# Earlier start of a triangular inverse's upper levels, other places for score products, and zero products inside its steps

## The chip, the cores and the metric

The kernel is one program on one core of a Trainium2 chip. It uses TensorE (PE: matrix products, results into the banks ps0 to ps7 of PSUM), VectorE (DVE), ScalarE (ACT), GpSimd (POOL), and SyncE (SP), which here only issues DMAs. The metric is the device time of one execution in microseconds, as the median of the runs. Lower is better.

## What is computed

Two transformer blocks over 256 tokens of width 1024. The change touches the mixer of the first block only, which has an RWKV-7 half and an attention half (NSA). Their outputs are put side by side and projected. All arithmetic is fp32; a projection is split in high and low parts (three products for one).

```python
def step(S, inp):                      # RWKV-7, one token, 8 heads of 64
    r_t, w_t, k_t, v_t, a_t, b_t = inp
    sa = jnp.einsum('bhvk,bhk->bhv', S, a_t)
    S = S * w_t[:, :, None, :] + sa[..., None] * b_t[:, :, None, :] + v_t[..., None] * k_t[:, :, None, :]
    return S, jnp.einsum('bhvk,bhk->bhv', S, r_t)
...
k_cmp = compress(kc, pe_k, ck1, ck2)   # gelu(blk @ w1) @ w2, 15 blocks
v_cmp = compress(vc, pe_v, cv1, cv2)
...
return gb[..., 0:1] * o_c + gb[..., 1:2] * o_s + gb[..., 2:3] * o_w
```

The scan over tokens is done in two chunks of 128 tokens. Within a chunk it needs, for each head, the inverse of a unit lower triangular matrix of 128 by 128 made of products of keys: 16 of them, called units of the inverse.

## The kernel before

**Front part.** `w_in` (L764) runs the items of the first projection in the order of `IN_ITEMS`: column blocks 0 to 21, then `gate`, then the two token products `tok 0` and `tok 1`. A column block waits for `lo_blk`, which VectorE gives with `lo_block` (L2034) after ScalarE's cast of the same block. Near the end VectorE also makes the keys `bT` and `kT_` (L2194 to L2197, semaphore `ab_ready`).

**Score products.** `rwkv_A_first` (L820) makes the strictly lower part of all 16 matrices into four banks, `rwkv_A(p)` (L833) the rest for the pair p of heads (p from 0 to 7). VectorE reads them through a mask: `A_first` (L2268), then `A_rest(lo, hi)` (L2283), one read for each of 16 matrices. A pair can only be made when an earlier pair's banks have been read (`A_read`). A table `A_PAIRS` tells behind which items pairs are made.

**The inverse.** SP moves the diagonal blocks of 16 by 16 through DRAM into a layout where VectorE inverts all of them at once (`small_inverse`, L2292), and back: one DMA out, then eight in (`blocks_back`). Levels 4, 5 and 6 then join blocks to 32, 64 and 128 rows. That is done in twelve steps (`STEPS`: three levels, four groups of four matrices). A step q is: P, eight small products into ps0 (`rwkv_P`, L853); a copy of P by ScalarE (`P_ev`); dM, small products into ps1 (`dM_ps`); an update of M by VectorE (`M_ready`) and, at level 4, transposes of M (`Mt_ready`). P of step q+1 is issued right behind dM of step q.

**The attention** is 34 units, software-pipelined in `nsa(i)`. TensorE's `nsa(i)` issues the scores of unit i, the value product of unit i-3 and the transpose of unit i-2; VectorE adds the bias and takes the maximum of unit i (L2358); ScalarE takes the exponential of unit i-1 and copies the transpose of unit i-2. Units 0 to 16 have 128 keys (short), 17 to 33 have 256 (long). Units 8 and 25 are the compressed branch, and behind units 7, 8, 16, 24 and so on VectorE makes a result (L2317).

**The compression.** `compress` (L1019) makes the hidden layer, `compress_T` turns it, ScalarE applies Gelu in `compress_act` (L1592), TensorE makes compressed keys and values in `compress_out` (L1049), ScalarE copies them, and VectorE's `compress` (L2396) spreads the values (`Vbd`, `cmp_ready`). The first transpose of the attention on TensorE waits for `cmp_ready`.

**The order in `rwkv`** (L872, L1518, L2201) is written out by hand for each engine. TensorE: pairs 4 and 5, `compress_T`, pair 6, `nsa(0)`, pair 7, `compress_out`, five zero products, `nsa(1)` to `nsa(3)` with four zero products behind each, and then P of step 0 and the steps. `stay_busy` issues the zero products: the operand is zero, and nobody reads the result. `NSA_STEPS` tells how many `nsa` calls a step holds.

## Time and profile before

| | us |
|---|---|
| median of 3 runs | 1398.94 (1398.36 to 1399.71) |
| the profiled execution | 1398.15 |
| its span in the profile | 1396.3 |
| TensorE busy | 1368.1 |
| VectorE busy | 943.5 |
| ScalarE busy | 689.1 |

The times in the rows count from the start of the span. Each engine carries out its instructions in order. The rows are from one execution, the profiled one. "x16" in a row of PE counts records, of which an fp32 product has two.

### The profile page before, as it was taken

Reading aid. Unit: us, or ns where it says so; the run is one execution under the profiler, and the core shown is the slowest. Engines: PE = TensorE matmul, PEld = TensorE weight load, DVE = VectorE, ACT = ScalarE, POOL = GpSimd, SP = SyncE. Lnnn points to the kernel's source line nnn. Section 1 sums busy time; section 2 is a strip of 40 time slices with the busy share of each in tenths; the row PEclk is TensorE's granted clock in tenths of the full one; section 3 lists DMA queues with packets and bytes.
Section 4 is the critical chain, followed back from the end, with each engine's and each line's share of the span. In section 5 each row is a group of like instructions: output and inputs, shape, how many; then the busy total and the mean of one; then the engine's idle time right before and its main releaser. Section 6 shows DMA issues by size and latency. Waiting matters only on the chain. (4 is left out here: it accounts for less than half of the span.)

```text
span 1396.3 us, 25767 instructions
## 1 busy us (share of the span) xinstructions
PE 1368.1 (98%) x10188; PEld 1261.5 (90%) x10188; DVE 943.5 (68%) x1539; ACT 689.1 (49%) x1107; POOL 82.3 (6%) x137
## 2 busy tenths in 40 slices
PE   8999999999999999999999999999999999999997
PEld 8897788999989999899989999999998988899997
DVE  4778567766668666577577666676665676676665
ACT  6764545433454443376654433444433756643442
POOL 1031010000020000000000000100000123000000
PEclk9999999999999999999999999999999999999999
DMA  9355015655536555433356555365555423465540
GB/s 360 137 170 189 2 34 224 226 180 192 205 106 227 219 181 185 177 116 129 119 210 228 195 180 188 133 232 203 193 180 181 151 92 137 181 226 182 197 162 31
DMA packets 33070, 239.48 MB, mean 172 GB/s; under 512 B 6864, under 2 KB 13280, under 8 KB 14304
## 3 DMA queue, kind: packets, MB, share of 16 engines
q1 hardware_dynamic: 30320, 234.84, 46.4%
q10 hardware_dynamic: 2672, 3.58, 0.8%
q8 instruction: 52, 0.85, 0.2%
q14 instruction: 26, 0.21, 0.0%
HBM read 236.15 MB, written 2.25 MB: 171 GB/s over the span
## 5 line engine op out<-in xcount | busy, mean ns | idle before, releaser
L500 PE MATMUL ps<-uT_h,w_gu 128*128 128x256 f32 x3520 | 600.2, 277 | 2.1 <-ACT uT_h L1335 2.0
L500 PEld LDWEIGHTS ps<-uT_h,w_gu 128*128 128x128 f32 x3520 | 532.7, 188 | 12.8 <-issue 4.7
L500 PE MATMUL ps<-uT_l,w_gu 128*128 128x256 f32 x1760 | 474.6, 277 | 0.0
L500 PEld LDWEIGHTS ps<-uT_l,w_gu 128*128 128x128 f32 x1760 | 325.3, 188 | 0.0
L500 PE MATMUL ps<-w_dn,h_r 128*128 128x512 f32 x1320 | 320.4, 392 | 0.3 <-DVE h_r L2089 0.3
L500 PEld LDWEIGHTS ps<-w_dn,h_r 128*128 128x128 f32 x1320 | 239.7, 188 | 46.7 <-issue 1.5
L1387 ACT CAST w_gu<-ring 128x2048 fp32r<-128x2048 f32 x110 | 209.9, 1908 | 139.5 <-PE ps L500 139.1
L2047 DVE TENSOR_TENSOR w_gu<-ring,w_gu 128x2048 fp32r<-128x2048 f32 x110 | 252.1, 2292 | 35.0 <-ACT w_gu L1387 35.0
L1400 ACT ACTIVATE wk<-wk 128x256 f32<-128x256 f32 x110 | 46.0, 418 | 265.6 <-DVE wk L2078 265.5
L2080 DVE TENSOR_TENSOR us<-ps,bc 128x256 f32<-128x256 f32 x110 | 46.5, 422 | 185.5 <-PE ps L500 185.5
L1393 ACT CAST w_dn<-ring 128x1024 fp32r<-128x1024 f32 x110 | 115.7, 1052 | 76.3 <-PE ps L500 75.7
L2053 DVE TENSOR_TENSOR w_dn<-ring,w_dn 128x1024 fp32r<-128x1024 f32 x110 | 134.1, 1219 | 5.1 <-ACT w_dn L1393 4.9
L500 PE MATMUL ps<-uT_h,ring_r 128*128 128x256 f32 x408 | 113.2, 279 | 0.0
L500 PEld LDWEIGHTS ps<-uT_h,ring_r 128*128 128x128 f32 x408 | 77.0, 189 | 0.6 <-issue 0.2
L500 PE MATMUL ps<-wk 32*32 32x32 f32 (+8 forms) x648 | 70.9, 273 | 2.3 <-DVE small L2358 1.0
L2078 DVE TENSOR_TENSOR wk<-ps,bc 128x256 f32<-128x256 f32 x110 | 46.7, 425 | 34.2 <-PE ps L500 20.9
L500 PE MATMUL ps<-ring_r,uT_h 128*128 128x512 f32 (+2 forms) x176 | 61.7, 351 | 0.0
L500 PEld LDWEIGHTS ps<-wk 128*128 128x128 f32 (+4 forms) x648 | 48.7, 160 | 9.2 <-issue 2.6
L2083 DVE TENSOR_TENSOR wk<-wk,us 128x256 f32<-128x256 f32 x110 | 46.8, 425 | 8.0 <-ACT wk L1400 4.8
L500 PE MATMUL ps<-uT_h,in_h 128*128 128x256 f32 x176 | 49.6, 284 | 1.8 <-DVE ring_r L2040 1.7
L2089 DVE TENSOR_TENSOR h_r<-wk,h_r 128x256 fp32r<-128x256 f32 x110 | 46.8, 426 | 3.8
L500 PE MATMUL ps<-uT_l,in_h 128*128 128x256 f32 x176 | 47.8, 278 | 0.0
(397 smaller groups left out, 1693.3 us busy)
## 6 DMA issues: line engine op xcount, KB each, us to landing
ring<-wstream SPq DMA_DIRECT2D x144, 1536.0 KB, 6.3
cst<-consts_in SPq DMA_DIRECT2D x1, 2185.0 KB, 13.7
wk<-t_row ACTq DMA_DIRECT2D x1, 2048.0 KB, 8.1
wk<-masks_in SPq DMA_DIRECT2D x1, 1216.0 KB, 24.0
x<-x_in SPq DMA_DIRECT2D x2, 512.0 KB, 4.7
ring<-wstream SPq DMA_DIRECT2D x1, 1024.0 KB, 8.8
inh<-gains ACTq DMA_DIRECT2D x2, 512.0 KB, 9.9
tri_blocks<-wk SPq DMA_DIRECT2D x3, 256.0 KB, 2.8
```

The costliest lines, as they stand in the source:

```text
L500: return pe.matmul(o, l, r, start=start, stop=stop, skip_group_check=True)
L1387: act.copy(w_gu[:, c % 2, 0, :], slot(i)[:, 0:2 * D]).then_inc(s["hi_a"], 1)
L1393: act.copy(w_dn[:, c % 2, 0, :], slot(i)[:, 2 * D:3 * D]).then_inc(s["hi_b"], 1)
L1400: act.activation(sg[:, c % 2, :], sg[:, c % 2, :], ACT.Silu).then_inc(s["silu_ready"], 1)
L2047: v.tensor_tensor(w_gu[:, c % 2, 1, :], slot(i)[:, 0:2 * D], w_gu[:, c % 2, 0, :].bitcast(F32), ALU.subtract).then_inc(s["lo_a"], 1)
L2053: v.tensor_tensor(w_dn[:, c % 2, 1, :], slot(i)[:, 2 * D:3 * D], w_dn[:, c % 2, 0, :].bitcast(F32), ALU.subtract).then_inc(s["lo_b"], 1)
L2078: v.tensor_tensor(h, ps[4 + c % 2][:, 0:T], bc[:], ALU.mult).then_inc(s["gs_ready"], 1)
L2080: v.tensor_tensor(us[:], ps[6 + c % 2][:, 0:T], bc[:], ALU.mult).then_inc(s["us_ready"], 1)
L2083: v.tensor_tensor(h, h, us[:], ALU.mult).then_inc(s["h_mul"], 1)
L2089: v.tensor_tensor(hr[:, 1, :], h, hr[:, 0, :].bitcast(F32), ALU.subtract).then_inc(s["h_ready"], 1)
```

## The change

In words:

- VectorE: `lo_block` 21 no longer stands between the products for column groups 3 and `bT`, but behind both products that make `bT`.
- TensorE: `rwkv_A_first` goes from behind `gate` to behind column 21. Pairs 0 and 1 are made behind `gate`, pair 2 in the middle of `tok 0`, pair 3 behind it, 4 and 5 behind `tok 1`, 6 and 7 inside the compression. Before, they were 0 and 1 behind `tok 0`, 2 and 3 behind `tok 1`, 4 to 7 behind the compression.
- VectorE: `small_inverse` stands behind the reads of eight matrices, not four.
- P of step 0 stands right behind the compression. `compress_T` stands behind it; `compress_out` behind P of step 1. On ScalarE `compress_act` and its part of `compress_out` stand behind the copy of step 0, on VectorE `compress` behind `nsa(2)`.
- No attention unit stands ahead of the steps. `NSA_STEPS` holds 32 calls, not 28.
- `stay_busy` issues two zero products in each of the eight steps of levels 4 and 5, into the unused half of ps1. The 17 zero products ahead of the steps are gone.

```diff
-        A_PAIRS = {("tok", 0): (0, 1), ("tok", 1): (2, 3)}
+        A_PAIRS = {("gate", 0): (0, 1), ("tok", 0): (3,), ("tok", 1): (4, 5)}
...
-        NSA_FIRST, NSA_STEPS, BRANCHES = 4, [2, 2, 2, 2, 3, 3, 2, 3, 3, 2, 2, 2], (1, 0, 2)
+        NSA_STEPS, BRANCHES = [2, 2, 2, 2, 3, 3, 3, 3, 3, 3, 3, 3], (1, 0, 2)
...
-            def stay_busy(n, bank):
-
-                for _ in range(n):
-                    mm(ps[bank][:, 0:P], zk[:, 2, :], zk[:, 2, :])
+            def stay_busy(o):
+
+                for _ in range(2):
+                    mm(o, zk[:, 2, :], zk[:, 2, :])
...
-                        last = tok_split("in", bank, 23, it[1], P, 3 * P)
+                        last = tok_split("in", bank, 23, it[1], P, 3 * P, {} if it[1] else {KC // 2: lambda: rwkv_A(2)})
...
-                    if it == ("gate", 0):
+                    if it == ("col", 21):
                         rwkv_A_first()
...
             def rwkv():
-                rwkv_A(4)
-                rwkv_A(5)
+                pe.wait_ge(s["A_read"], A_FIRST_READ + 13)
+                rwkv_P(0)
                 pe.wait_ge(s["tok_ev"], 4)
                 pe.wait_ge(s["cmp_row"], 1)
                 compress_T()
-                rwkv_A(6)
-                nsa(0)
-                rwkv_A(7)
-                compress_out()
-                pe.wait_ge(s["A_read"], A_FIRST_READ + 14)
-                stay_busy(5, 0)
                 pe.wait_ge(s["A_read"], A_FIRST_READ + RWKV_UNITS)
-                for i in range(1, NSA_FIRST):
-                    nsa(i)
-                    stay_busy(4, 0)
-                i = NSA_FIRST
-                rwkv_P(0)
+                i = 0
                 for q, (lv, k) in enumerate(STEPS):
                     nsa(i)
                     i += 1
-                    pe.wait_ge(s["P_ev"], q + 1)
                     if q:
                         pe.wait_ge(s["M_ready"], q)
+                    if lv < 6:
+                        stay_busy(ps[1][:, 256:384])
+                    pe.wait_ge(s["P_ev"], q + 1)
...
+                    if q == 0:
+                        compress_out()
...
+                    if m in (11, 14):
+                        rwkv_A(6 if m == 11 else 7)
...
             def rwkv():
-                compress_act(0)
-                compress_act(1)
-                act.activation(small[:, 61:62], C("neg_half", 0, 1), ACT.Exp)
-                nsa(0)
-                compress_out()
-                for i in range(1, NSA_FIRST):
-                    nsa(i)
-                i = NSA_FIRST
+                i = 0
                 for q in range(len(STEPS)):
                     act.wait_ge(s["P_ps"], q + 1)
                     A(act.copy(Pb[:, q % 2, 0:256], ps[0][:, 0:256]), "P_ev")
+                    if q == 0:
+                        compress_act(0)
+                        compress_act(1)
+                        act.activation(small[:, 61:62], C("neg_half", 0, 1), ACT.Exp)
+                        compress_out()
...
-                    if c % 2:
-                        lo_block("in", 20 + c // 2)
+                    if c == 1:
+                        lo_block("in", 20)
                 V(v.tensor_tensor(bT, kk, agm, ALU.mult))
                 V(v.tensor_tensor(bT, bT, E2, ALU.mult))
+                lo_block("in", 21)
...
                 A_first()
-                A_rest(0, 4)
+                A_rest(0, 8)
                 small_inverse()
-                A_rest(4, 14)
-                nsa(0)
-                A_rest(14, 16)
-                compress()
-                for i in range(1, NSA_FIRST):
-                    nsa(i)
-                i = NSA_FIRST
+                A_rest(8, 16)
+                i = 0
...
+                    if q == 1:
+                        compress()
```

Three places in the order of the engines. The first is on VectorE, near the end of the projection, before the change: L2040 is `lo_block` (here 21), L2194 and L2195 make `bT`, L2197 makes `kT_`.

```order
L2191 TENSOR_TENSOR wk<-wk 128x2x128 [waits v_step]
L2040 TENSOR_TENSOR ring_r<-ring,in_h 128x8x128 [waits hi_blk,v_step]
L2194 TENSOR_TENSOR wk<-wk,xn 128x1024
L2195 TENSOR_TENSOR wk<-wk 128x1024 [waits v_step]
L2197 TENSOR_TENSOR wk<-wk 128x1024 [waits e_ready,v_step]
```

The same place on VectorE with the change, where line numbers are four lower:

```order
L2187 TENSOR_TENSOR wk<-wk 128x2x128 [waits v_step]
L2190 TENSOR_TENSOR wk<-wk,xn 128x1024 [waits v_step]
L2191 TENSOR_TENSOR wk<-wk 128x1024 [waits v_step]
L2036 TENSOR_TENSOR ring_r<-ring,in_h 128x8x128 [waits hi_blk,v_step]
L2194 TENSOR_TENSOR wk<-wk 128x1024 [waits e_ready]
```

`lo_block` 21 moved behind the two products for `bT`.

The second is on TensorE, right behind `compress_out`, before the change: zero products (misc), scores, values and transposes of units 1 to 3, and P of step 0 (64x32).

```order
L500 MATMUL ps<-misc 128x128 [waits A_read]
L500 MATMUL ps<-misc 128x128 x4
L500 MATMUL ps<-wk 128x128 [waits A_read]
L500 MATMUL ps<-misc 128x128 x4
L500 MATMUL ps<-wk 128x128 [waits max_ready]
L999 MATMUL ps<-cst,wk 128x128 [waits cmp_ready,p_ready]
L500 MATMUL ps<-misc 128x128 x4
L500 MATMUL ps<-wk 128x128 [waits max_ready]
L500 MATMUL ps<-misc,wk 128x64 [waits cmp_ready,gate_tok,npT_ev]
L999 MATMUL ps<-cst,wk 128x128 [waits p_ready]
L500 MATMUL ps<-misc 128x128 x4
L500 MATMUL ps<-wk 64x32 [waits blocks_back]
```

The same engine with the change, from P of step 0: `compress_T` (128x33), score 0, two zero products, dM of step 0, P of step 1, `compress_out` (hid, cst).

```order
L500 MATMUL ps<-wk 64x32 x7
L1043 MATMUL ps<-cst,wk 128x33 [waits cmp_row,tok_ev]
L1043 MATMUL ps<-cst,wk 128x33 x3
L500 MATMUL ps<-wk 128x128 [waits A_read]
L500 MATMUL ps<-misc 128x128 x2
L500 MATMUL ps<-wk 64x32 [waits Mt_ready,P_ev]
L500 MATMUL ps<-wk 64x32 x7
L500 MATMUL ps<-wk 64x32 [waits P_ev,blocks_back]
L500 MATMUL ps<-wk 64x32 x7
L500 MATMUL ps<-hid,cst 128x32 [waits cmp_hact]
```

P of step 0 moved ahead of `compress_T`, and `compress_out` behind P of step 1; units 0 to 3 moved behind both.

The third is on ScalarE at the same place, before the change: L1590 copies the hidden row, L1595 and L1599 are `compress_act`, L1521 loads the Exp table.

```order
L1590 COPY wk<-ps 97x256 [waits tok_ev,cmp_h]
L1595 COPY small<-ps 128x1 [waits cmp_hT,cmp_row]
L1595 COPY small<-ps 128x1 [waits a_step]
L1599 ACTIVATE hid<-ps,small 128x32 [waits a_step] x2
L1595 COPY small<-ps 128x1 [waits cmp_hT,a_step]
```

With the change:

```order
L1586 COPY wk<-ps 97x256 [waits tok_ev,cmp_h]
L1520 COPY wk<-ps 128x256 [waits P_ps,cmp_row]
L1591 COPY small<-ps 128x1 [waits cmp_hT,P_ev]
L1591 COPY small<-ps 128x1 [waits a_step]
L1595 ACTIVATE hid<-ps,small 128x32 [waits a_step] x2
```

The copy of P of step 0 (L1520) moved ahead of `compress_act`.

## Rows read from the trace of the kernel before

**Rows 1.** Page, busy time of TensorE's products and weight loads, span share, instructions.

```profile
PE 1368.1 (98%) x10188; PEld 1261.5 (90%) x10188; DVE 943.5 (68%) x1539; ACT 689.1 (49%) x1107; POOL 82.3 (6%) x137
```

**Rows 2.** Stretches from:to, busy us by engine (instructions), granted clock, DMA share, GB/s.

```profile
113.50:119.60 6.10, 5.34 (x50) 3.85 (x48) 5.55 (x12) 3.79 (x12) 0.00 (x0) 1.00 0.43 56
...
140.50:147.40 6.90, 6.48 (x61) 5.52 (x62) 3.41 (x17) 3.62 (x16) 0.00 (x0) 0.51 0.02 4
...
155.90:169.90 14.00, 13.94 (x125) 11.31 (x125) 8.88 (x29) 7.67 (x27) 0.00 (x0) 1.00 0.01 1
```

**Rows 3.** The same view in quarters of a microsecond, at both ends of the half clock.

```profile
140.50:140.75 0.25, 0.00 (x0) 0.00 (x0) 0.22 (x2) 0.00 (x0) 0.00 (x0) 0.76 0.00 0
...
147.25:147.50 0.25, 0.25 (x2) 0.10 (x1) 0.01 (x1) 0.24 (x2) 0.00 (x0) 0.58 0.00 0
```

**Rows 4.** Order in time, VectorE: start, us, engine, line, operation [idle before].

```profile
86.94 1.23 DVE L2040 TENSOR_TENSOR ring_r<-ring,in_h 128x1024 fp32r<-128x1024 f32 x1 [1.42 <-ACT in_h L1373]
88.08 1.22 DVE L2194 TENSOR_TENSOR wk<-wk,xn 128x1024 f32<-128x1024 f32 x1
```

**Rows 5.** Order in time, small_inverse and its DMAs, and the eight copies' landing.

```profile
104.98 0.38 DVE L2299 COPY wk<-wk 128x256 f32<-128x256 f32 x1 [2.48 <-DMA wk<-tri_blocks]
...
112.30 0.33 SPq L459 DMA_DIRECT2D inv_blocks<-wk  x1
113.98 3.77 SPq L465 DMA_DIRECT2D wk<-inv_blocks  x8
...
DMA to landing us min/median/max: 2.0/2.2/2.4
```

**Rows 6.** Order in time, TensorE behind the compression: pair 4, compress_out, zero products, P.

```profile
113.57 0.93 PE L500 MATMUL ps<-wk 64*128 64x128 f32 x8
...
118.37 0.63 PE L500 MATMUL ps<-hid,cst 128*128 128x32 f32 x4
...
119.64 1.38 PE L500 MATMUL ps<-misc 128*128 128x128 f32 x10
...
124.70 1.07 PE L500 MATMUL ps<-wk 64*64 64x32 f32 x18
```

**Rows 7.** Order in time, ScalarE: compress_act, the Exp table, the first softmax.

```profile
115.92 0.35 ACT L1595 COPY small<-ps 128x1 f32<-128x1 f32 x2 [1.76 <-PE ps L1045]
...
118.11 1.28 ACT L1521 ACT_TABLE_LOAD   x1
...
120.14 0.40 ACT L1572 ACTIVATE wk<-wk,small 128x128 f32<-128x128 f32 x1
```

**Rows 8.** Order in time, VectorE: Vbd, then updates of M, steps 0 to 4 and 8.

```profile
120.60 0.69 DVE L2399 TENSOR_TENSOR inh<-ps,small 128x512 f32<-128x512 f32 x1
...
126.76 0.43 DVE L2230 COPY_PREDICATED wk<-msk,ps 128x256 f32<-128x256 uint8 x1 [0.56 <-PE ps L500]
...
129.42 0.43 DVE L2230 COPY_PREDICATED wk<-msk,ps 128x256 f32<-128x256 uint8 x1
...
133.01 0.43 DVE L2230 COPY_PREDICATED wk<-msk,ps 128x256 f32<-128x256 uint8 x1
...
137.12 0.43 DVE L2230 COPY_PREDICATED wk<-msk,ps 128x256 f32<-128x256 uint8 x1
...
140.90 0.28 DVE L2222 COPY wk<-ps 32x128 f32<-32x128 f32 x1
...
156.68 0.42 DVE L2234 COPY wk<-ps 64x256 f32<-64x256 f32 x1 [1.05 <-PE ps L500]
```

**Rows 9.** Order in time, TensorE: short scores at half clock, long scores, first right-hand product.

```profile
140.92 0.79 PE L500 MATMUL ps<-wk 128*128 128x128 f32 x2 [0.95 <-DVE small L2358]
...
142.29 0.64 PE L500 MATMUL ps<-wk 128*128 128x128 f32 x2
...
153.12 0.60 PE L500 MATMUL ps<-wk 128*128 128x256 f32 x2
...
154.46 0.60 PE L500 MATMUL ps<-wk 128*128 128x256 f32 x2
...
169.87 2.38 PE L500 MATMUL ps<-wk 128*128 128x64 f32 x18
```

More of the change, by code:

```diff
@@ L753, in col_split, with tok_split @@
                 return last
-            def tok_split(kind, bank, blk, t, lo, hi):
+            def tok_split(kind, bank, blk, t, lo, hi, between={}):
                 w = parts(kind, blk)
                 for k in range(KC):
+                    if k in between:
+                        between[k]()
                     for n, (a, b) in enumerate(PASSES):
```

## Prediction

> **What bounds the kernel now.** I read the page first: TensorE (PE in the rows) is busy for 1368 of 1396 us [rows 1]. So the end moves only with time that TensorE spends idle, on products nobody needs, or at a low clock. The change touches about 90 us around the end of the first projection; everything behind it is the same code. The second view is therefore the busy time of the engines in the stretches of that stage [rows 2]. What to see in it: from 113.5 to 119.6 TensorE has 0.8 us idle; from 140.5 to 147.4 it runs at a granted clock of 0.51; from 155.9 to 169.9 it is busy for 13.94 of 14.00 us. The finer stretches place that drop: half clock (1.2 GHz) from the quarter behind 140.5 on, full again in the quarter behind 147.25 [rows 3]. Before the drop TensorE had begun to stand still, for 0.95 us up to 140.92 [rows 9].
>
> The third view is the order in time of the engines. The twelve upper steps of the inverse (a step is P, its copy on ScalarE, dM, an update of M on VectorE) begin at 124.92, right behind one score product at 124.70 [rows 6], while the blocks they need have landed at about 119.5: the last of eight copies is issued at 117.3 and lands after 2.2 us [rows 5]. So 5.4 us lie between. They are filled with attention units 0 to 3 and 17 zero products, the first of them at 119.64 [rows 6].
>
> **The front part: two moves on VectorE.** lo_block 21 is what column 21 waits for. It starts at 86.94, after 1.42 us of idle time that VectorE spends on ScalarE's cast [rows 4]. Now two products of 1.26 us each (start to start) go ahead, from 85.56, so it starts at 88.08 and column 21 starts 1.1 us later: +1.1 us on TensorE. In return kT_ is ready 1.3 us earlier, at 90.5 and not 91.8; nothing covers the +1.1, since TensorE has no other item to take.
>
> The score products (A_first, then pairs 0 to 7) are the same number at other places, no cost of their own. What they move is small_inverse. It began at 104.98 behind a 2.48 us wait for the gathered blocks [rows 5]. A_first now stands behind column 21, so its reads end 1.8 us earlier and the gather could be in at 103.2; but pair 3 stands behind the whole of token product 0, at about 102.2, and VectorE must read pair 3 first (1.06 us to its first read, then two reads of 0.6), so small_inverse starts at 104.5. It takes 7.3 us, since SP writes the inverses out at 112.30 [rows 5]: the blocks are back at 119.0 instead of 119.5. Of the SP queue nothing else is moved.
>
> TensorE now meets P of step 0 behind the compression: the compression ended at 113.57 [rows 6]; add 3.0 for pairs 4 to 7, which now lie ahead or inside (8 records in 0.93 and two pairs with little more, 0.75 a pair), and the 1.1 of the front: 117.6. It waits there for the blocks, 1.4 us idle. P starts at 119.2, 5.7 us earlier than before.
>
> **What stands behind that P.** The transposes of the hidden layer are behind it on TensorE, and on ScalarE its copy stands ahead of compress_act. So the compression's chain starts at 120.2 and not at 115.92 [rows 7]. It takes 2.2 us to the last Gelu (118.10), so compress_out on TensorE can start at 122.65, where it was 118.37 [rows 6, 7]. Its products take 1.27 us (118.37 to 119.64). The Exp table load of 1.28 us and its activation run beside them. The first softmax of the attention was at 120.14; now it is 124.8. Then one more obstacle: on TensorE the first transpose of the attention waits for cmp_ready, and VectorE computes that only behind score 2, whose product needs the maximum of score 1. Score 1 starts at 124.0, its maximum is out at 125.0, score 2 is read by 126.0, and the Vbd product (0.28 and 0.69 us, the latter at 120.60 in [rows 8]) ends at 127.05. dM of step 1 is queued behind that transpose: 127.7 with the two zero products. Its update of M falls at 128.5; before it fell at 129.42 [rows 8]. So of the 5.7 us won at the start of the steps 0.9 is left at step 1, and by then three units of attention are issued, not seven.
>
> The Trainium skill, "ScalarE: Activation LUTs", section "What ACT_TABLE_LOAD costs", says that a switch of tables costs 1.28 us and a drain of about 1.38 us beside it. In this trace the load starts at 118.11, directly behind the Gelu, and takes 1.28 us [rows 7]; with the page's drain the first softmax would come up to 1.4 us later and so would the end. I keep the trace.
>
> **The steps.** Updates of M before were at 126.76, 129.42, 133.01, 137.12, 140.90 and, for step 8, 156.68 [rows 8]. The bare step with two short units costs 2.66; TensorE now has two zero products more in it (0.24 each, from ten records in 1.22 us [rows 6]), which brings it to about 2.75. The compressed unit adds 0.9 (133.01 less 129.42 less 2.66), the first result 1.45, the second 1.85, all on VectorE. After: step 1 at 128.5, steps 2 and 3 at 131.3 and 134.0, step 4 (with the compressed unit) at 137.3, step 5 with both results behind it 4.9 later at 142.2, steps 6 and 7 at 3.0 and 3.3 each (0.8 for dM and P, 0.5 for zero products, 0.5 a short unit), step 8 at 152.8 after three long scores. That is 3.9 us ahead of 156.68. But the new plan has issued 20 units there, the old one 23. A long unit costs 1.34 us (153.12 to 154.46 [rows 9]), TensorE issuing without a gap, so three cost 4.0. Behind this point both plans hold the same work. Net of the steps: +0.1 us.
>
> A count of TensorE's time from the compression's end to the first product behind the steps, at 169.87 [rows 9], gives +1.1 instead. Before, 56.3 us less 3.0 for pairs; of that about 43.4 is needed work, so 9.9 is lost: 1.3 in stalls between the pairs, 4.0 in zero products, 4.6 in VectorE's hold and the half clock. After: from 117.6, 1.4 + 3.9 idle up to 127, 3.8 in 16 zero products, 1.2 in VectorE's hold at step 5 come to 10.3, on a start that is 1.1 later with 0.3 for rounding. I take the middle of +0.1 and +1.1: **+0.6 us**, if the clock stays at full.
>
> **The clock.** It will not. Between 117.6 and 127.1 TensorE has 4.2 us of work, mostly small tiles; before the drop at 140.5 it had stood still for less than a microsecond. I expect half clock from about 120 to 127, as long as the stretch before (6.8 us). Of TensorE's work there only a part is on the chain: 0.25 for the transposes, 1.0 for compress_out, 0.4 for scores 1 and 2, 0.2 for the zero products, so **+1.8 us**. The bounds: 0 if it stays at full; for a stretch that lasts 7 us longer, steps at half clock (short units start at 140.92 and 142.29 [rows 9], 1.37 us apart where 0.5 do at full clock) cost 2.1 each more: two units at 0.85 and 0.4 for the zero products.
>
> The Trainium skill, "TensorE: Matmul & The Clock Gate", section "A second HAM failure mode: psum-queue depth-cycling", says that short idle gaps between groups of matmuls are enough to make the clock swing between its levels. By that rule the zero products would not hold the clock in the steps. It is the mechanism of the second rival below.
>
> **Sum.** +0.6 and +1.8 is +2.4 us. The profiled execution took 1398.15 us (1396.3 of span and 1.85 around it), so 1400.6 for its like; its time lies 0.8 below the median of 1398.94, and by the median the forecast is **1401.3 us**. That is 0.17%. A difference within 0.2% (2.8 us) can't be told from none in a measurement of this kernel; so this is a forecast of no change, on the slow side.
>
> **Rivals.**
> First, faster: the chain of the steps sets the end and not TensorE's total. Then the three late units fit into waits of the steps and their 4.0 us are not paid, nor the clock's 1.8 in the steps: 0.1 less 4.0 is -3.9, 1395.0 us. For it: TensorE stood still for a microsecond before 140.92, and lost about 2.9 us to the half clock of 140.5 to 147.4, which zero products in the steps may prevent. Against it: 13.94 busy of 14.00 us at the end [rows 2]. It decides if dM of steps 7 to 11 waits for M and not for its turn.
> Second, slower: the clock stays at half, or comes back only when TensorE is fully busy, through steps 1 and 2. Each costs 2.1 us more, with half of a second one hidden: +5.2, 1404.1 us. It decides from 127 on; for it speaks that before, with 6.48 us of work in 6.90, the clock came back only at the end of that stretch [rows 2].
> Third, the clock does not fall at all at 120: +0.6, 1399.5 us.
>
> **How the numbers follow.** Forecast 0.42, faster 0.20, slower 0.28, clock kept 0.10. Faster than 1396.1: nearly all of the first rival, 0.19. Above 1401.7: the second rival and a quarter of the forecast's own spread (1399.8 to 1403.0), 0.38. Within: 0.43. The range takes in both rivals' values up to a tenth at each end: 1395.0 to 1404.6.
>
> **What would show it.** In the profile after: column 21 a microsecond later; P of step 0 at about 119 behind 1 to 2 us of idle TensorE; compress_out at 122 to 124; the first attention transpose waiting for Vbd, at 127 to 129; a granted clock near 0.5 from about 120; the step 8 update at 152 to 155 and the first right-hand product at 171 to 173. If that product comes before 168, the first rival is right; if half clock reaches beyond 131, the second.

## The result and the profile after

| | before | after |
|---|---|---|
| median, us | 1399.10 (1397.48 to 1405.10, 20 executions) | 1408.59 (1401.70 to 1413.58, 20 executions) |
| ratio of after to before, 95% interval | | 1.0063 [1.0051, 1.0076] |
| the profiled execution, us | 1398.15 | 1401.70 |

The change makes the kernel slower by 0.63%. The forecast of 1401.3 us was 7.3 us too low, and the time lies outside its range. The profiled execution of after is the fastest of its twenty: that one profile looks as if the forecast had been right. What sets it apart is the last number of an execution, its mean granted clock. Here it is 0.996, and 17 of the 20 executions have 0.986 to 0.992. The three with 0.996 took 1401.70 to 1402.96 us, the seventeen 1407.13 to 1413.58. The lost part of the clock, times two, times the span, is the time spent at half clock: 0.996 is 11 us of it (in the profiled execution 6.8 in this stage and 4.3 at the very end), 0.990 is 28 us. Before has 0.993 to 0.998 in the executions that ran beside the experiments.

The rows of the profiled execution of after. TensorE's products take the same time as in [rows 1]:

```profile
PE 1367.8 (98%) x10186; PEld 1259.5 (90%) x10186; DVE 942.7 (67%) x1539; ACT 689.5 (49%) x1107; POOL 84.3 (6%) x137
```

Order in time, VectorE; these answer to [rows 4, 5]. lo_block 21 stands behind the two products, and small_inverse begins without any idle time ahead of it:

```profile
87.74 1.22 DVE L2036 TENSOR_TENSOR ring_r<-ring,in_h 128x1024 fp32r<-128x1024 f32 x1
88.89 1.22 DVE L2194 TENSOR_TENSOR wk<-wk 128x1024 f32<-128x1024 f32 x1
...
104.83 0.39 DVE L2293 COPY wk<-wk 128x256 f32<-128x256 f32 x1
```

Order in time, TensorE, to be held against [rows 6, 9]: P of step 0 (released by the landing of the inverse blocks), compress_out, scores 1 and 2, and the first transpose of the attention, for which TensorE waits 1.75 us for VectorE's Vbd:

```profile
119.24 0.66 PE L500 MATMUL ps<-wk 64*64 64x32 f32 x16 [0.66 <-DMA wk<-inv_blocks]
...
122.62 0.63 PE L500 MATMUL ps<-hid,cst 128*128 128x32 f32 x4 [0.57 <-ACT hid L1595]
...
123.89 0.71 PE L500 MATMUL ps<-wk 128*128 128x128 f32 x4
126.35 0.45 PE L995 MATMUL ps<-cst,wk 128*128 128x128 f32 x1 [1.75 <-DVE inh L2393]
...
173.58 2.38 PE L500 MATMUL ps<-wk 128*128 128x64 f32 x18
```

The last row is the first right-hand product, the end of the twelve steps: 169.87 before, 173.58 here. I use its start as the yardstick for every kernel below, since everything behind it is the same code.

Stretches of one microsecond, TensorE alone (from:to, length, busy us, granted clock, DMA share, GB/s), at both ends of the half clock in this execution:

```profile
125.00:126.00 1.00, 0.00 (x0) 0.97 1.03 442
126.00:127.00 1.00, 0.65 (x3) 0.50 0.95 406
...
131.00:132.00 1.00, 1.00 (x5) 0.50 0.98 418
132.00:133.00 1.00, 1.00 (x12) 0.62 0.96 397
```

It falls inside the wait for Vbd and lasts 6.8 us, as long as in [rows 3]. The question is what the other 17 executions do.

### The profile page after: what moved, and what is told of

The parts are those of the page before. It is cut to its first block and busy times, and to the rows that moved or that the text cites. A ratio compares the mean times of both kernels' runs of the same rounds, so it can differ in the third digit from the quotient of the medians.

```text
span 1399.9 us, 25764 instructions
## 1 busy us (share of the span) xinstructions
PE 1367.8 (98%) x10186; PEld 1259.5 (90%) x10186; DVE 942.7 (67%) x1539; ACT 689.5 (49%) x1107; POOL 84.3 (6%) x137
```

## Experiments

One table first. "Half clock" is what the profiled execution shows between 112 and 160 us. "Right-hand product" is the start of the yardstick row there. "Mean clocks" are those of all executions of the kernel. The ratios are against executions of the kernel before on the same chip, beside those of the run; the medians come from several chips and are not to be compared across them. The second and third columns are of one execution each.

| kernel | half clock, us | right-hand product | mean clocks | median, us | ratio [95%] |
|---|---|---|---|---|---|
| before | 140.6 to 147.5, 6.8 | 169.87 | 0.993 to 0.998 | 1399.10 | 1 |
| after | 125.9 to 132.8, 6.8 | 173.58 | 17 of 20 at 0.986 to 0.992 | 1408.59 | 1.0063 [1.0051, 1.0076] |
| e1_after | 124.9 to 148.8, 23.9 | 179.60 | 4 of 5 at 0.989 to 0.990 | 1408.66 | 1.0056 [1.0031, 1.0080] |
| e2_no_zero | 123.2 to 147.1, 23.9 | 177.24 | 0.986 to 0.990 | 1406.51 | 1.0053 [1.0031, 1.0076] |
| e3_fill | none | 170.93 | 0.997 to 0.999 | 1403.93 | 1.0020 [1.0002, 1.0037] |
| e4_before_zeros | 142.0 to 148.8, 6.8 | 171.85 | 0.995 to 0.999 | 1405.60 | 1.0026 [1.0007, 1.0046] |
| e5_fill_only | 144.4 to 154.6, 10.2 | 173.62 | 0.993 to 0.999 | 1401.80 | 1.0000 [0.9981, 1.0020] |
| e6_reorder | 144.1 to 154.4, 10.2 | 173.05 | 0.989 to 0.997 | 1404.77 | 1.0027 [1.0005, 1.0049] |
| e7_front_back | 124.9 to 138.6, 13.7 | 176.05 | 0.988 to 0.996 | 1408.42 | 1.0045 [1.0023, 1.0066] |
| e8_dense | 123.3 to 137.0, 13.7 | 179.80 | 0.993 to 0.998 | 1409.09 | 1.0033 [1.0014, 1.0052] |
| e9_fill_late_zeros | none | 170.19 | 0.995 to 0.999 | 1399.28 | 1.0003 [0.9987, 1.0019] |
| e10_fill_T | none | 170.72 | 0.996 to 0.999 | 1398.96 | 1.0000 [0.9985, 1.0015] |
| e11_fill_P | 128.7 to 149.2, 20.5 | 179.02 | 5 of 6 at 0.990 to 0.992 | 1408.82 | 1.0057 [1.0035, 1.0079] |
| e12_before_no_zeros | 120.8 to 144.7, 23.9 | 172.35 | 0.986 to 0.992 | 1402.46 | 1.0030 [1.0011, 1.0048] |
| e13_early_Vbd | 125.9 to 149.8, 23.9 | 178.88 | 6 of 7 at 0.988 to 0.991 | 1408.78 | 1.0065 [1.0038, 1.0092] |
| e14_early_fill | 121.9 to 128.7, 6.8 | 171.24 | 11 of 12 at 0.995 to 0.998 | 1402.01 | 1.0016 [1.0005, 1.0027] |

The medians of e3_fill and e4_before_zeros look too high for their right-hand products. The last section shows what was longer in their profiles.

### The kernel after once more: e1_after

> The changed kernel once more, unchanged, for a second traced execution beside the first. The first took 1401.7 us (span 1399.9), but the median of twenty is 1408.6, at a mean granted clock of about 0.990 and not 0.996. Theory 'clock': another execution has half clock for much longer, 14 us or more in sum behind 117 us, and the steps at half clock between 120 and 145; a clock 0.005 lower over 1400 us is 14 us more at half clock and costs about 7 us. Rival 'elsewhere': the additional half clock lies behind 190 us, in stretches that the change does not touch. Rival 'work': the time grows at full clock.

Here is the long stretch, in stretches of TensorE (columns as above):

```profile
124.50:138.10 13.60, 12.31 (x109) 0.51 0.68 287
138.10:150.00 11.90, 11.90 (x144) 0.55 0.01 1
```

VectorE's updates of M in steps 1 to 5:

```profile
128.20 0.43 DVE L2224 COPY_PREDICATED wk<-msk,ps 128x256 f32<-128x256 uint8 x1 [2.02 <-PE ps L500]
...
133.42 0.43 DVE L2224 COPY_PREDICATED wk<-msk,ps 128x256 f32<-128x256 uint8 x1 [2.37 <-PE ps L500]
...
138.64 0.43 DVE L2224 COPY_PREDICATED wk<-msk,ps 128x256 f32<-128x256 uint8 x1 [2.37 <-PE ps L500]
...
144.46 0.44 DVE L2219 COPY_PREDICATED wk<-msk,ps 128x256 f32<-128x256 uint8 x1
...
151.39 0.44 DVE L2219 COPY_PREDICATED wk<-msk,ps 128x256 f32<-128x256 uint8 x1
```

Up to 125 us the rows are those of the first profile of after, some 0.5 us earlier as a whole (lo_block 21 at 87.25, P of step 0 at 118.69); then the clock falls ahead of the first transpose as there, and stays down for 23.9 us instead of 6.8. In the second of the two stretches TensorE is busy for all of its 11.90 us, and the clock still comes back only at 148.8. The right-hand product comes 9.7 us later than before, and the medians differ by 8.9 to 9.5. So the whole excess lies in this stage, and it is the clock.

### Which gap drops it: e3_fill, e10_fill_T, e11_fill_P

TensorE idles at three places there: 0.66 us ahead of P of step 0, 0.57 ahead of compress_out, 1.75 ahead of the first attention transpose. Zero products fill all three, the last, or the first two.

```diff
+                stay_busy(ps[0][:, 0:P], 4)        # e3, e11
                 rwkv_P(0)
...
                     if q == 0:
+                        stay_busy(ps[2][:, 0:P], 3)    # e3, e11
                         compress_out()
...
                     u, a = i - 2, units[i - 2]
+                    if u == 0:
+                        stay_busy(ps[2][:, 0:P], 9)    # e3, e10
                     pe.wait_ge(s["p_ready"], u + 1)
```

> The changed kernel with 16 more zero products where its trace shows TensorE idle: 4 ahead of P of step 0, 3 ahead of compress_out, 9 ahead of the first attention transpose. They lie in 0.7, 0.6 and 1.75 us of idle time and cost at most 1 us. Theory 'clock': the idle stretch is what brings the clock down, so it stays up in most executions and the median falls by 4 to 9 us against the changed kernel's, to 1400 to 1404. Rival 'steps': the clock falls in the steps for want of work there, so nothing or 1 us is won.

> The kernel after with one fill only: 9 zero products ahead of the first attention transpose, where TensorE stands idle for 1.75 us at 124.6. It tells which of the idle stretches drops the clock. If the last and longest one does, the clock stays at full in most executions (mean 0.996 or more, median near e3_fill's 1403.9). If the idle stretches at 118 to 119 and 122 count as well, the fall comes all the same at 124 to 126, and as a fall there lasts 7 to 24 us, most executions have a mean clock of 0.993 or less and the median is 1406 or more. I hold the first for likelier: in the kernel after the granted clock fell inside that stretch.

> The kernel after with the other two fills only: 4 zero products ahead of P of step 0 and 3 ahead of compress_out; TensorE still waits 1.75 us for Vbd ahead of the first attention transpose. By the theory that this last wait drops the clock, nothing changes against the kernel after: half clock from about 125, mean clock 0.993 or less in most executions, median 1408 to 1409. By the rival, that it takes all three idle stretches together, the clock stays at full and the median is near 1403.

In e10_fill_T the nine zero products run together with scores 1 and 2 and the transpose follows at once. The clock stays at full (third block, columns as above), and the updates of M come in full-clock steps:

```profile
124.20 2.17 PE L500 MATMUL ps<-misc 128*128 128x128 f32 x18
126.21 0.27 PE L997 MATMUL ps<-cst,wk 128*128 128x128 f32 x1
```

```profile
127.63 0.43 DVE L2226 COPY_PREDICATED wk<-msk,ps 128x256 f32<-128x256 uint8 x1 [1.13 <-PE ps L500]
...
130.74 0.43 DVE L2226 COPY_PREDICATED wk<-msk,ps 128x256 f32<-128x256 uint8 x1 [0.53 <-PE ps L500]
...
133.85 0.43 DVE L2226 COPY_PREDICATED wk<-msk,ps 128x256 f32<-128x256 uint8 x1 [0.52 <-PE ps L500]
...
137.33 0.45 DVE L2221 COPY_PREDICATED wk<-msk,ps 128x256 f32<-128x256 uint8 x1
...
142.51 0.44 DVE L2221 COPY_PREDICATED wk<-msk,ps 128x256 f32<-128x256 uint8 x1
```

```profile
124.50:138.10 13.60, 13.20 (x214) 1.00 0.70 295
138.10:150.00 11.90, 10.77 (x165) 1.00 0.02 3
```

e11_fill_P, with the first two gaps filled and the third left, falls at 128.7 and is as slow as after:

```profile
126.66 0.30 PE L997 MATMUL ps<-cst,wk 128*128 128x128 f32 x1 [1.75 <-DVE inh L2395]
```

```profile
128.00:129.00 1.00, 1.00 (x20) 0.84 1.04 442
...
149.00:150.00 1.00, 1.00 (x44) 0.92 0.00 0
```

So nine zero products in the third gap bring the ratio from 1.0063 to 1.0000 with no execution below a mean clock of 0.996, and filling the other two alone changes nothing (1.0057). That shows the fall of the clock in this part to be the cause. It does not tie the fall to the third gap: in e11_fill_P it came 2 us behind it, and in the profiles of e2_no_zero, e8_dense and e14_early_fill ahead of it, at 121.9 to 123.3. In e8_dense the clock fell in a microsecond in which TensorE was busy throughout, half a microsecond behind an idle stretch of 0.57 us:

```profile
123.00:124.00 1.00, 1.00 (x8) 0.65 1.02 430
```

Held against each other, e1_after and e10_fill_T also price it. From one update of M to the next, steps 1 to 5: 5.22, 5.22, 5.82, 6.93 us at half clock, 3.11, 3.11, 3.48, 5.18 at full. The differences are 2.11, 2.11, 2.34 and 1.75, together 8.3; 0.6 us of lateness was there at step 1. That is the 8.9 us between the right-hand products, 179.60 and 170.72. Nothing of it was hidden.

### Is it the wait or the lack of work: e13_early_Vbd, e14_early_fill

The wait can be taken away by order, without a zero product: Vbd behind the first update of M, ahead of the reads of scores 1 and 2.

```diff
                         V(v.transpose(Mt[:, qs, :], Mm[:, qs, :]), "Mt_ready")
+                    if q == 0:
+                        compress_v()      # the two instructions that make Vbd
                     for _ in range(NSA_STEPS[q] - 1):
```

> The kernel after with the cause of the wait taken away instead of the wait filled: on VectorE the product Vbd stands right behind the first update of M (121.7), ahead of the reads of scores 1 and 2, and no zero product is added. Vbd is then done at about 123.9 instead of 126.2, and the first attention transpose waits for the first softmax (begun at 124.59) instead, so TensorE's idle stretch ahead of it shrinks from 1.75 to about 0.5 us. If it is the length of that one stretch that drops the clock, the clock stays at full in most executions (mean 0.996 or more), the update of M of step 1 comes 1 us earlier than 128.76 and the median is within 0.2% of the kernel before. If it takes dense work there, as the zero products of e10_fill_T gave it, the clock falls all the same and the median is 1405 or more.

The wait shrank as planned, the transpose came 1 us earlier, and the clock fell all the same:

```profile
124.10 0.71 PE L500 MATMUL ps<-wk 128*128 128x128 f32 x4
125.36 0.33 PE L995 MATMUL ps<-cst,wk 128*128 128x128 f32 x1 [0.55 <-ACT wk L1568]
```

```profile
125.00:126.00 1.00, 0.64 (x5) 0.96 1.03 442
...
149.00:150.00 1.00, 1.00 (x42) 0.59 0.00 0
```

The theory that this one idle stretch does it by its length has fallen. What e10_fill_T gave TensorE was 2.2 us of full products in place of the wait; e13_early_Vbd only closed up small ones.

> As e13_early_Vbd, with 5 zero products ahead of the first attention transpose and the two of each step only in steps 4 to 7 (1.0 us less of them than in the kernel after). If the steps up to 5 are a chain whose start counts, the 1 us of the earlier Vbd comes on top of e9_fill_late_zeros: executions without other disturbance at 1396.5 to 1397.5 and a median 0.5 to 1 us below the kernel before of the same chip. If TensorE's total counts, it ends where e9_fill_late_zeros does (1.0003 times before, 1398 to 1399).

e14_early_fill adds 5 zero products to that order. 11 of its 12 executions keep a mean clock of 0.995 or more, but the profiled one still falls, at 121.9, ahead of them. At 1.0016 it is not better than e9_fill_late_zeros (1.0003). Whether the earlier transpose brings anything stays open: in the one profile half clock had made it late (127.58).

### What zero products in the steps do: e2_no_zero, e5_fill_only, e9_fill_late_zeros, e8_dense

e2_no_zero is after without the two lines in the steps; e5_fill_only is e3_fill without them; e9_fill_late_zeros is e3_fill with them in steps 4 to 7 only; e8_dense is after with six instead of two in steps 1 to 5:

```diff
-                    if lv < 6:
-                        stay_busy(ps[1][:, 256:384])     # e2, e5
+                    if 4 <= q < 8:
+                        stay_busy(ps[1][:, 256:384])     # e9
+                    if lv < 6:
+                        stay_busy(ps[1][:, 256:384], 6 if 1 <= q <= 5 else 2)   # e8
```

> The changed kernel without the two zero products in the eight steps of levels 4 and 5. Theory 'clock': they hold the clock up in the steps, so without them the clock is lower still and the median 2 to 6 us above the changed kernel's. Rival 'cost': the clock falls anyway because of the idle stretch ahead, the zero products only take TensorE's time: 1 to 3 us faster than the changed kernel.

> The kernel after with the fills of e3_fill (4 zero products ahead of P of step 0, 3 ahead of compress_out, 9 ahead of the first attention transpose) and without the two zero products of each step. My theory: the idle stretch ahead of step 1 is what drops the clock, and the zero products of the steps only cost their own time. So there is no half clock before 150, M of step 8 updates near 153 and M of step 11 near 167.3 (e3_fill 169.26, less the 2 us that e2_no_zero saved against e1_after), the first residual of the next stage comes 1.2 us ahead of the kernel before and the median is near 1401.9 (e3_fill 1403.9). Rival, the zeros hold: once the steps have no zero products their gaps drop the clock as they did in the kernel before at 140.5; then a half-clock stretch of 7 to 20 us stands between 127 and 150, M of step 11 comes at 169 or later and the median is 1403 or more.

> The kernel after with the three fills of e3_fill, and the two zero products only in steps 4 to 7 instead of 0 to 7. e3_fill (zero products in all eight) had no half clock, e5_fill_only (in none) had it from 144.3 to 154.3, where its steps 5 to 7 lie. My theory: zero products are worth their 0.13 us each only where gaps would let the clock fall, so this kernel keeps full clock (mean granted clock 0.998 or more in most executions) for 1.0 us of zero products instead of 2.1; M of step 11 near 168.3, an execution with no other disturbance 1399 to 1400, about 1 us below e3_fill's 1400.4, and the median within 0.2% of the kernel before. Rival: one run of e3_fill and one of e5_fill_only differ by chance and the zero products of the steps hold nothing; then half clock stands between 140 and 155 here too, mean clock 0.993 to 0.996, M of step 11 at 171 to 172, no better than e5_fill_only.

> The kernel after with six zero products instead of two in each of steps 1 to 5, 20 more in all, which cost 20 x 0.13 = 2.6 us at full clock if they find no gap. My theory: once the clock is down it comes back only behind TensorE work without gaps, so filling the gaps of the steps brings it back early, before 135 instead of 148.8, which saves up to 6 us of e1_after's 9.4: the median is 1403 to 1407. Rival, a fixed length: the half clock lasts as long as it lasts, whatever is issued; then it still ends near 148 in the executions where it does so now, and the median is 1410 to 1413.

Once the clock is down, two zero products in a step did not shorten the stretch (23.9 us with them and without, one profile each) and were not free: the right-hand product of e2_no_zero is 2.4 us earlier without the sixteen, though its P of step 0 is 0.8 us later (119.50 against 118.69). While the clock is at full they do hold it. e5_fill_only without them falls behind a wait of 1.09 us in step 5:

```profile
143.38 0.49 PE L500 MATMUL ps<-wk 128*128 128x128 f32 x2 [1.09 <-DVE small L2354]
```

```profile
143.00:144.00 1.00, 0.49 (x2) 1.00 0.00 0
144.00:145.00 1.00, 0.94 (x28) 0.69 0.00 0
154.00:155.00 1.00, 1.00 (x6) 0.69 0.00 0
```

It is the fall of the kernel before at 140.5 [rows 3, 9]. In e3_fill the same wait is 0.52 us, with zero products ahead of the group and behind it, and there is no fall. Of the mean clocks of e5_fill_only five of twelve are 0.995 or less; of e3_fill's ten none is below 0.997. e9_fill_late_zeros keeps them only there: right-hand product at 170.19, no half clock. In the times the held clock does not show: e5_fill_only has 1.0000, e3_fill 1.0020 and e9_fill_late_zeros 1.0003, and the intervals overlap. My guess that the wait alone decides is too simple, by e13_early_Vbd.

Six in a step (e8_dense) end it early by the mean clocks: all ten are 0.993 or more where after has 17 of 20 below. The profile alone (to 137.0) would not show it, since e7_front_back without them has a stretch of 13.7 us too. A fixed length is refuted: 6.8, 13.7, 20.5 and 23.9 us all occur. But nothing was gained by it. The profiled execution is the slowest of its ten, with the lowest mean clock, and its right-hand product (179.80) is as late as that of e1_after; against e7_front_back, at the same length of half clock, the twenty further zero products made it 3.8 us later (176.05). The median, 1409.09, lies in neither expected range and is no better than that of e7_front_back beside it, 1408.42; the ratios, 1.0033 and 1.0045, overlap.

### The kernel before: e12_before_no_zeros, e4_before_zeros

```diff
                 pe.wait_ge(s["A_read"], A_FIRST_READ + 14)
-                stay_busy(5, 0)
...
                     nsa(i)
-                    stay_busy(4, 0)
```

> The kernel before without its 17 zero products between 119.6 and 124.7. They stood in front of P of step 0, where the inverse blocks had landed at about 119.5. My theory, from the kernel after: without them TensorE has gaps there of the kind that dropped the clock after the change, so the clock falls at 120 to 125 in most executions, M of step 0 comes earlier (about 124.5 to 125.5 instead of 126.8) but the steps run at half clock, the mean clock is 0.993 or less in most executions and the median is 1402 to 1408. Rival: the zero products of the kernel before are only a cost of 17 x 0.13 = 2.2 us; then the clock is at full until 138, the mean stays at 0.996 and the median falls by 1 to 2 us below the kernel before.

All twelve executions have a mean clock of 0.986 to 0.992: without its 17 zero products the kernel before has the same fault.

```profile
120.00:121.00 1.00, 0.35 (x2) 0.92 1.01 418
...
144.00:145.00 1.00, 1.00 (x43) 0.63 0.00 0
```

So the 17 zero products of [rows 6], which I had booked as 4.0 us lost, were what kept the clock; the change took them out, where TensorE has least to do, and put 16 in where they are worth little.

> The kernel before with one part of the change alone: two zero products in each of the eight steps of levels 4 and 5. If the half clock of 140.5 to 147.4 comes from too little work in the steps, they keep it up: 1 to 2 us faster. If they only cost time on TensorE: 1 to 3 us slower.

e4_before_zeros is the kernel before with two zero products more in each of the first eight steps. The right-hand product moves from 169.87 to 171.85, 2.0 us for 16 of them, and in the profile the stretch of 6.8 us stays. Two of the ten executions have a mean clock of 0.999 and took 1398.43 and 1400.19 us, the other eight 0.995 to 0.996 and 1404.75 to 1406.93: so in two of ten the zero products may have held the clock here too, but no profile shows such an execution.

### The front part and the order of the compression: e7_front_back, e6_reorder

> The kernel after with one part undone: lo_block 21 stands again ahead of the two products with bT, where the kernel before has it. My theory: column 21 comes 1.1 us earlier, P of step 0 too (118.1) unless the blocks are late, and as all behind it moves as one the median is 1.1 below the kernel after, 1407.5; the half clock stays as it is, 7 to 24 us from about 124. Rival: the 1.1 us is covered, because TensorE waits for the inverse blocks ahead of P of step 0 anyway; then P of step 0 stays at 119.2 behind 1.7 us of idle time instead of 0.66, and the median stays at 1408.6. A lower time by more than 3 us would say that the order in the front sets the length of the half clock.

```diff
-                    if c == 1:
-                        lo_block("in", 20)
+                    if c % 2:
+                        lo_block("in", 20 + c // 2)
...
                 V(v.tensor_tensor(bT, bT, E2, ALU.mult))
-                lo_block("in", 21)
```

The clock makes the times useless for 1.1 us (1.0045 [1.0023, 1.0066] against 1.0063 and 1.0056). In the trace A_first now waits 0.59 us for kT_, the first pairs 0.83 us for VectorE's reads, and P of step 0 still waits for the blocks:

```profile
91.62 2.06 PE L500 MATMUL ps<-wk 64*128 64x128 f32 x32 [0.59 <-DVE wk L2193]
...
97.36 1.58 PE L500 MATMUL ps<-wk 64*128 64x128 f32 x16 [0.83 <-DVE wk L2273]
...
119.54 0.66 PE L500 MATMUL ps<-wk 64*64 64x32 f32 x16 [0.55 <-DMA wk<-inv_blocks]
```

From the start of lo_block 20 to P of step 0 it takes 38.2 us here (81.38 to 119.54) and 37.9 in e1_after (80.81 to 118.69). So the 1.1 us is covered, but not as that rival had it. It expected 1.7 us of idle time ahead of P of step 0, and there are 0.55, as in e1_after (0.59). What is won on column 21 is lost at once: in this order kT_ comes behind lo_block 21, so A_first has to wait for it. From lo_block 20 to the first pairs it takes 16.0 us here (to 97.36) and 15.7 in e1_after (to 96.47).

> As e5_fill_only, and the compression's chain is put ahead: the transposes of the hidden layer before P of step 0 on TensorE, half of the Gelus before the copy of P on ScalarE, and Vbd behind the first update of M on VectorE, not behind score 1 of the attention; 3 and 4 zero products where 4 and 9 stood. My theory: the first attention transpose (126.35 in the kernel after, 1.75 us of it waiting for Vbd) comes near 124.5 and M of step 1 updates near 126.3; the steps are a chain until about step 5, so M of step 11 comes 1 to 1.5 us ahead of e5_fill_only and the median is 1 to 1.5 below it, near 1400.5, which is level with the kernel before or a little under it. Rival: TensorE's total sets the end of the steps; then what is won at step 1 is given back as fewer long score products have been issued, and the median is within 0.5 of e5_fill_only less the 6 zero products that went (0.13 each, 0.8 us).

e6_reorder put the transposes of the hidden layer ahead of P of step 0; they then waited 0.77 us for ScalarE's copy and delayed that P. The first attention transpose came at 127.06, not at the 124.5 that was planned, and the update of M of step 1 at 128.04, 0.53 us ahead of e5_fill_only. The right-hand product comes 0.57 us ahead of it. That fits a chain whose start counts as well as TensorE's total with six zero products fewer (expected 0.8), so this run does not decide between the two. Its ratio (1.0027 against 1.0000) gives no gain at all.

## Why the prediction was wrong, by its own steps

**Front part, the small inverse, P of step 0: right.** lo_block 21 predicted at 88.08, measured 87.74, in an execution whose rows there lie 0.3 us early. small_inverse: 104.5 predicted, 104.83 measured. P of step 0: 119.2 and 119.24. TensorE reached that P at 118.58, not at 117.6, and so idled 0.66 us and not 1.4; the landing of the blocks hid that miss. Wrong is "nothing covers the +1.1": the earlier kT_ covers it, since with the old order A_first waits for kT_ and the pairs for its reads (e7_front_back).

**What stands behind that P: right, and not read to its end.** compress_out 122.65 predicted and 122.62 measured, the first softmax 124.8 and 124.59, the wait for Vbd there as forecast, Vbd's end 127.05 predicted and 126.20 measured (scores 1 and 2 ran back to back, where I had let score 2 wait for the maximum of score 1). On the table load the measurement decides against the Trainium skill, "ScalarE: Activation LUTs", section "What ACT_TABLE_LOAD costs": the load of 1.28 us has no drain of about 1.38 us beside it after the change either:

```profile
121.80 0.77 ACT L1595 ACTIVATE hid<-ps,small 128x128 f32<-128x128 f32 x2
122.58 1.28 ACT L1524 ACT_TABLE_LOAD   x1
123.88 0.20 ACT L1524 ACTIVATE small<-cst 128x1 f32<-128x1 f32 x1
```

**The steps at full clock: right.** The sum said +0.6 us. e10_fill_T, which is the change at full clock with nine zero products in a wait, has its right-hand product 0.85 us behind before, between the two ways of counting (+0.1 and +1.1), and its ratio at 1.0000. Step 8 was predicted at 152.8 and came at 153.8 there. The first rival, faster, is refuted by the same row: the three late units are paid.

**The clock: the step that failed, twice.** The term of +1.8 us for the clock was mis-sized; by the traces it is 8.9 us in e1_after, whose mean clock 17 of the 20 executions of after share within 0.004. First the length. "I expect half clock from about 120 to 127, as long as the stretch before (6.8 us)" took the length of another fall as that of this one. It fell at 125, which was no great miss, but the return was at 148.8 in e1_after. Secondly the place. Of 6.8 us only 1.8 were put on the chain; e10_fill_T against the first profile of after gives 2.9 (173.58 less 170.72), and the whole stretch costs 8.9. Behind 127 every product of a step at half clock is on the chain.

**The second rival** was the right mechanism at too small a size. Its price, 2.1 us a step, was measured to the tenth, 2.11. It was charged to two steps with half of one hidden, +5.2 in all (the terms as written, 2.4 and 2.1 and half of 2.1, give 5.6, which changes nothing here); it was four steps, 2.11, 2.11, 2.34 and 1.75, with nothing hidden. So the upper end of the range, 1404.6, lay 4.0 us below the measured 1408.59. What would end the stretch was the question to ask, and the trace of before did not hold the answer: it has one such fall, of 6.8 us. The condition that I gave this rival, that the clock comes back when TensorE is fully busy, does not describe e1_after either: 11.90 us busy of 11.90, and half clock for the first 10.7 of them. Here the Trainium skill, "TensorE: Matmul & The Clock Gate", section "A second HAM failure mode: psum-queue depth-cycling", was nearer than my forecast: it lets short gaps between groups of matmuls swing the clock. The traces agree: the idle stretches ahead of the falls last 0.37 to 1.75 us. What I had drawn from it, that two zero products in a step would not hold the clock, fits e2_no_zero against e1_after for a clock that is down (23.9 us both) and differs from e3_fill against e5_fill_only for one that is up.

**The zero products.** I costed the removed 17 as a gain of 4.0 us and never asked what they covered. e12_before_no_zeros answers it: they had kept the clock.

## What stays open

Why the same instructions bring a stretch of 6.8 us in one execution of after and 23.9 in another. Up to the fall the two profiles differ by a shift of half a microsecond only. Which idle stretch brings the fall: it came between 121.9 and 128.7 in kernels that share these gaps. What ends a stretch, beyond that six zero products in each step shortened it by the mean clocks (e8_dense). And what exactly e13_early_Vbd lacks against e10_fill_T: the runs say that a shorter wait was not enough and dense products were, on one place. No version beat the kernel before: e9_fill_late_zeros (1.0003 [0.9987, 1.0019]) and e10_fill_T (1.0000 [0.9985, 1.0015]) equal it.

## What to carry to other kernels

Zero products in a thin stretch of TensorE are not waste until a run without them says so: seventeen here took 4.0 us of TensorE's time and held off 24 us at half clock, and without them the kernel was slower (1.0030). Price a fall of the clock by what one step loses at half clock (2.1 us here) times all the steps of the thin stretch behind it, at least as the other end of the range, not by the length of one fall seen elsewhere. And look at the mean clock of all executions before trusting one profile: the profiled one here was the best of twenty.

## What the runs showed of the hardware

**The same code, a whole stage 2% slower.** The medians of e3_fill and e4_before_zeros are above what their right-hand products say by 3 to 4 us. In their profiles one of the seven stages between residual sums takes about 4.1 us longer than in before, in code that the edits don't touch, at full granted clock. Groups by line (form, count, busy us, mean ns, idle before), the same stage in before and in e4_before_zeros:

```profile
L500 PE MATMUL ps<-uT_h,w_gu 128*128 128x256 f32 x704 | 120.1, 277 | 0.1
L500 PE MATMUL ps<-uT_l,w_gu 128*128 128x256 f32 x352 | 94.9, 277 | 0.0
```

```profile
L500 PE MATMUL ps<-uT_h,w_gu 128*128 128x256 f32 x704 | 123.9, 281 | 0.1
L500 PE MATMUL ps<-uT_l,w_gu 128*128 128x256 f32 x352 | 96.5, 281 | 0.0
```

Each of the 1056 products takes 281 ns instead of 277, from the first to the last of the stage; the stages behind it lose at most 0.5 us each. It happened in other stages too (in e3_fill and e11_fill_P the last one, in e8_dense the fourth, in e14_early_fill the fifth, and in e13_early_Vbd the same as here). The executions of before lie mostly at 1397 to 1400, with a second group at 1402 to 1405, as if one stage had it. Only profiled executions show the stage, so that it explains the medians is likely and not shown, and what triggers it stays open.

**The clock costs 0.37 to 0.43 us for each us at half.** Against e10_fill_T, 8.9 us for 23.9 and 2.9 for 6.8, in a stage in which TensorE waits for other engines part of the time.
